# Handing parts of the norms between ScalarE, VectorE, GpSimd and TensorE, and a one-pass second layer norm, in a two-block transformer kernel

## The reference

```python
# block 1, per layer (mod is made from c by ada_w and ada_b)
h = rmsnorm(x, norm_mix_g[l]) * (1.0 + sc1) + sh1
u = h @ w_in[l]
...
x = x + g1 * (mix @ w_out[l])
h = rmsnorm(x, norm_ffn_g[l]) * (1.0 + sc2) + sh2
f = (jax.nn.silu(h @ ffn_w1[l]) * (h @ ffn_w3[l])) @ ffn_w2[l]
x = x + g2 * f
...
# after block 1
x = rmsnorm(x, final_g)
# block 2, per layer
h = x @ w_in[i]
...
x = layer_norm(ALPHA * x + mix, ln1_g[i], ln1_b[i])
gate, up = jnp.split(x @ w_ffn_in[i], 2, axis=-1)
ffn = (jax.nn.silu(gate) * up) @ w_ffn_out[i]
ple = (p[i] @ w_ple[i]) * jax.nn.sigmoid(x @ w_ple_gate[i])
x = layer_norm(ALPHA * x + ffn + ple, ln2_g[i], ln2_b[i])
```

## Time and profile before

| | us |
|---|---|
| time of the kernel before, median of 3 runs | 2750.97 (2750.26 to 2753.71) |
| the profiled execution, its own time | 2746.25 |
| span of that execution in the profile | 2744.5 |
| PE busy (share of the span) | 2579.8 (94%) |
| POOL busy | 1126.8 (41%) |
| DVE busy | 1019.1 (37%) |
| ACT busy | 893.6 (33%) |

### The profile page before, as it was taken

The page is one execution under the profiler, slowest core; times in us unless marked ns, Lnnn a source line. Parts: engine busy times, 40 slices in busy tenths (PEclk is TensorE's granted clock), DMA queues, the critical chain, the costliest instruction groups (busy, mean ns, idle before and its releaser), DMA issues.

```text
span 2744.5 us, 30543 instructions
## 1 busy us (share of the span) xinstructions
PE 2579.8 (94%) x11680; PEld 2029.1 (74%) x11680; DVE 1019.1 (37%) x1750; ACT 893.6 (33%) x1177; POOL 1126.8 (41%) x388
## 2 busy tenths in 40 slices
PE   6897799999999779999989989999989998999998
PEld 4673688878776468887878668887868776888785
DVE  5683710039675560000059543000026846100002
ACT  4224332222423342222243553232124364222212
POOL 1332345544333225554425335555342633455441
PEclk8998899999999889999999999999999999999998
DMA  7511423257420333222322112322341211322231
GB/s 262 184 48 46 160 78 100 92 151 224 135 90 31 107 108 107 92 87 85 101 82 79 53 62 93 106 93 77 95 116 48 84 45 64 101 97 92 83 94 53
DMA packets 309325, 267.76 MB, mean 98 GB/s; under 512 B 20104, under 2 KB 298360, under 8 KB 308984
## 3 DMA queue, kind: packets, MB, share of 16 engines
q1 hardware_dynamic: 309240, 266.63, 30.9%
HBM read 264.51 MB, written 2.10 MB: 97 GB/s over the span
## 4 chain that ended last, share of the span: by engine, by line
PE 85%; DVE 5%; ACT 3%; issue 3%; POOL 2%; DMA 1%; SPq 1%; DVEq 0%; ACTq 0%; POOLq 0%
PE bank L2106 25%; PE bank L2108 25%; PE bank L2107 25%; POOL w_lo L1301 1%; PE bank L2200 1%; PE bank L2440 1%; PE bank L2350 1%; PE bank L2319 1%; PE bank L2506 1%; DMA z_a<-in_ada_w 1%; ACT w_hi L808 1%; DMA raw<-in_ffn_w 1%; PE bank L2539 1%; PE bank L2366 1%; DVE b_acc L1525 0%
## 5 line engine op out<-in xcount | busy, mean ns | idle before, releaser
L1301 POOL TENSOR_TENSOR w_lo<-raw,w_hi 128x2048 fp32r<-128x2048 f32 (+1 forms) x216 | 915.4, 4238 | 1188.6 <-ACT w_hi L808 1162.2
L2106 PE MATMUL bank<-h_hi,w_lo 128*128 128x512 f32 (+1 forms) x2192 | 871.2, 397 | 58.6 <-DVE h_lo L1590 25.1
L2107 PE MATMUL bank<-h_lo,w_hi 128*128 128x512 f32 (+1 forms) x2192 | 862.0, 393 | 0.0
L2108 PE MATMUL bank<-h_hi,w_hi 128*128 128x512 f32 (+1 forms) x2192 | 861.7, 393 | 0.0
L2106 PEld LDWEIGHTS bank<-h_hi,w_lo 128*128 128x128 f32 (+1 forms) x2192 | 416.4, 190 | 163.3 <-issue 55.0
L808 ACT ACTIVATE w_hi<-raw 128x2048 fp32r<-128x2048 f32 (+1 forms) x216 | 378.1, 1750 | 478.0 <-PE bank L2108 449.6
L2108 PEld LDWEIGHTS bank<-h_hi,w_hi 128*128 128x128 f32 (+1 forms) x2192 | 415.9, 190 | 89.7 <-issue 0.4
L2107 PEld LDWEIGHTS bank<-h_lo,w_hi 128*128 128x128 f32 (+1 forms) x2192 | 417.2, 190 | 87.1 <-issue 1.1
L1630 DVE TENSOR_TENSOR f_full<-f_act,bank 128x512 f32<-128x512 f32 x88 | 60.5, 688 | 883.8 <-PE bank L2108 883.8
L2106 PE MATMUL bank<-f_hi,w_lo 128*128 128x512 f32 x704 | 280.7, 399 | 13.3 <-POOL f_lo L1313 13.3
L2108 PE MATMUL bank<-f_hi,w_hi 128*128 128x512 f32 x704 | 280.8, 399 | 0.0
(11 more groups left out here) (305 smaller groups left out, 2455.4 us busy)
## 6 DMA issues: line engine op xcount, KB each, us to landing
raw<-in_ffn_w SPq DMA_DIRECT2D x44, 1024.0 KB
raw<-in_w_ffn_in SPq DMA_DIRECT2D x44, 1024.0 KB
raw<-in_w_in SPq DMA_DIRECT2D x34, 1024.0 KB
raw<-in_ffn_w SPq DMA_DIRECT2D x32, 704.0 KB
raw<-in_w_ffn_out SPq DMA_DIRECT2D x32, 704.0 KB
b_raw<-in_ada_w SPq DMA_DIRECT2D x16, 1024.0 KB, 5.1
a_raw<-in_ada_w SPq DMA_DIRECT2D x32, 512.0 KB, 4.7
z_a<-in_ada_w SPq DMA_DIRECT2D x4, 2048.0 KB, 13.3
```

The costliest lines, as they stand in the source:

```text
L1301: pool.tensor_tensor(b.w_lo[p][:, 0:n], b.raw[p][:, 0:n], b.w_hi[p][:, 0:n].bitcast(F32), ALU.subtract)\
L2106: pe.matmul(out, wlo, xhi, start=start, stop=False)
L2107: pe.matmul(out, whi, xlo, start=False, stop=False)
L2108: return pe.matmul(out, whi, xhi, start=False, stop=stop)
```

## The change

What follows names parts by letters.

(a) The counting semaphore of the low halves is now one for each slot, so that two engines can make them. At five norms, the `w_lo` of the unit p = 1 of the pair that follows is made by DVE (`dve_split`) and no longer by POOL: at the mid norm of each layer of block 1, at the end of each of its layers (where the next layer or block 2 begins), and at the end of layer 0 of block 2. POOL keeps p = 0.

(b) In the RMS norms DVE squares the last tile (`dve_square`) and ACT only tiles 0 to 6, so ACT's split of the unit p = 1 no longer stands behind a square.

(c) DVE no longer adds the last square; TensorE adds it by a second product with ones that accumulates in the same bank (`pe_rms`).

(d) The full value of tile 0 is made by DVE (`dve_full`, in layer norms `dve_normed`) and no longer by ACT.

(e) At the start of layer 1 of block 1, TensorE does the two parameter transposes first, then 4 of the 16 one-column products of part 0, then the two products of the norm, then the other 12 and the 16 of part 1.

(f) In ln1, TensorE adds the last tile into the mean by a second product; DVE adds up only to tile 6.

(g) ln2 is made in one pass (`dve_shift_norm`, `act_shift_norm`, `pe_shift_sums`, `pe_shift_norm`). After tile 3, DVE's sum goes to TensorE, and every tile is shifted by 2/D times that sum, a guess of the mean. The squares of the shifted tiles are made on ACT and summed on DVE while TensorE still multiplies w2. After the last tile, TensorE adds the last tile to the sum and the last square to the sum of squares, and the variance is the mean square less the square of the mean. The tiles are centred after that, each before it is scaled. The eight products over squares of line 2440 are gone for ln2. TensorE's loop over w2 is written out for its last half in block 2 (`down`), with one product with ones inside and two before the last unit.

Waits of a few operations on their own engine are counted on fewer semaphores; the instructions stay the same there.

```diff
-        self.lo = up("lo", 0, 2)
+        self.lo = [up(f"lo{p}", 0, 1) for p in range(2)]
...
         act.activation(b.h_hi[:, k, :], b.sq[:, k, :], ACT.Identity, bias=bias, scale=gain[:, k:k + 1])\
            .then_inc(s.hh.up, 1)
-        act.activation(full[:, k, :], b.sq[:, k, :], ACT.Identity, bias=bias, scale=gain[:, k:k + 1])\
-           .then_inc(s.hf.up, 1)
+        if k:
+            act.activation(full[:, k, :], b.sq[:, k, :], ACT.Identity, bias=bias, scale=gain[:, k:k + 1])\
+               .then_inc(s.hf.up, 1)
...
-        if i == 7:
-            act_next(act, e, after, 0)
-        act_square(act, e, l * 2 + 2, i, w2_square(b, i), lay.bank_out(i % 2, Q_W2 + i // 2))
-        if i == 7:
-            act_next(act, e, after, 1)
+        if i < 7:
+            act_square(act, e, l * 2 + 2, i, w2_square(b, i), lay.bank_out(i % 2, Q_W2 + i // 2))
+        else:
+            for p in range(2):
+                act_next(act, e, after, p)
...
+def act_shift_norm(act, e, l, low):
+
+    s, b, bank = e.s, e.b, e.bank
+    act.wait_ge(*s.n2_mean(l, 2))
+    act.activation(b.f_full[:, 1, :], bank[6][:, :], ACT.Square, scale=1.0 / D).then_inc(s.n2_r.up, 1)
+    act.wait_ge(*s.n2_var(l, 1))
+    act.activation(b.r[:, :], b.f_full[:, 1, :], ACT.Ln, bias=b.eps[:, 1:2]).then_inc(s.n2_r.up, 1)
+    act.wait_ge(*s.n2_r(l, 2))
+    act.activation(b.r[:, :], b.r[:, :], ACT.Exp, scale=-0.5).then_inc(s.n2_r.up, 1)
+    act_normed(act, e, l * 2 + 1, 16, low)
...
+def dve_square(dve, e, k, out, ready):
+
+    dve.wait_ge(*ready)
+    dve.tensor_tensor(out, e.b.x[:, k, :], e.b.x[:, k, :], ALU.mult).then_inc(e.s.ssq.up, 1)
+
+
+def dve_split(dve, e, u):
 
     s, b = e.s, e.b
-    dve.wait_ge(*s.r(c, 1))
+    dve.wait_ge(*s.hi_in(u, 1))
+    dve.tensor_tensor(b.w_lo[1][:, :], b.raw[1][:, :], b.w_hi[1][:, :].bitcast(F32), ALU.subtract)\
+       .then_inc(s.lo[1].up, 1)
+
+
+def dve_full(dve, e, c, gain, shift, full):
+
+    s, b = e.s, e.b
+    dve.wait_ge(*s.xr(c, KD if c == 0 else 1))
+    if shift is None:
+        op = dve.tensor_scalar(full[:, 0, :], b.sq[:, 0, :], gain[:, 0:1], None, ALU.mult)
+    else:
+        op = dve.tensor_scalar(full[:, 0, :], b.sq[:, 0, :], gain[:, 0:1], shift[:, 0:1], ALU.mult, ALU.add)
+    op.then_inc(s.xr.up, 1)
...
+def dve_shift_norm(dve, e, lay, l, low):
+
+    s, b, bank = e.s, e.b, e.bank
+    turn = 2 * DEPTH + 1 + l
+
+    def take(k):
+        dve.wait_ge(*s.tile(lay.pair(20 + k), 1, 1))
+        if k >= 5:
+            dve.wait_ge(*s.n2_d(l, k + 1))
+        dve.tensor_tensor(b.x[:, k, :], bank[k % 2][:, :], b.x[:, k, :], ALU.add).then_inc(s.bank[k % 2].up, 1)
+
+    def add_up(k, first, n):
+
+        if k == first:
+            dve.tensor_tensor(b.r[:, :], b.x[:, 0, :], b.x[:, 1, :], ALU.add).then_inc(s.n2_sum.up, 1)
+        else:
+            dve.wait_ge(*s.n2_sum(l, n))
+            dve.tensor_tensor(b.r[:, :], b.r[:, :], b.x[:, k, :], ALU.add).then_inc(s.n2_sum.up, 1)
+
+    def shift(k):
+        if k < 5:
+            dve.wait_ge(*lay.bank_out(k % 2, Q2_W2 + k // 2))
+        dve.scalar_tensor_tensor(b.x[:, k, :], bank[6][:, :], -2.0 / D, b.x[:, k, :], ALU.mult, ALU.add)\
+           .then_inc(s.n2_d.up, 1)
+
+    def centre(k):
+        dve.scalar_tensor_tensor(b.x[:, k, :], bank[6][:, :], -1.0 / D, b.x[:, k, :], ALU.mult, ALU.add)\
+           .then_inc(s.n2_c.up, 1)
+
+    def squares(k):
+        dve_rms_sum(dve, e, turn, k, b.f_full[:, 0, :], w2_square(b, k))
+
+    for k in range(5):
+        take(k)
+        if 1 <= k < 4:
+            dve.wait_ge(*lay.bank_out(k % 2, Q2_W2 + k // 2))
+            add_up(k, 1, k - 1)
+    dve.wait_ge(*s.n2_mean(l, 1))
+    for k in range(KD):
+        shift(k)
+    for k in range(1, 5):
+        dve.wait_ge(*s.n2_d(l, k + 1))
+        squares(k)
+        add_up(k, 1, k + 2)
+    for k in range(5, KD - 1):
+        take(k)
+        dve.wait_ge(*lay.bank_out(k % 2, Q2_W2 + k // 2))
+        add_up(k, 1, k + 2)
+        squares(k)
+    take(KD - 1)
+    dve_square(dve, e, KD - 1, w2_square(b, KD - 1), lay.bank_out(1, Q2_W2 + 3))
+    if low:
+        dve_split(dve, e, Layer(s, 2, l + 1).pair(0))
+    dve.wait_ge(*s.n2_r(l, 1))
+    dve.wait_ge(*s.rms(turn, 1))
+    dve.scalar_tensor_tensor(b.f_full[:, 1, :], bank[7][:, :], 1.0 / D, b.f_full[:, 1, :], ALU.mult, ALU.subtract)\
+       .then_inc(s.n2_var.up, 1)
+    for k in range(2):
+        centre(k)
+    dve.wait_ge(*s.n2_r(l, 3))
+    for k in range(KD):
+        dve.wait_ge(*s.n2_c(l, k + 1))
+        dve_scaled(dve, e, k)
+        if k == 0:
+            dve_normed(dve, e, l * 2 + 1, 16)
+        if k + 2 < KD:
+            centre(k + 2)
+        if low and k > 1:
+            dve_normed_low(dve, e, l * 2 + 1, k - 2)
+    if low:
+        dve_normed_low(dve, e, l * 2 + 1, KD - 2)
+        dve_normed_low(dve, e, l * 2 + 1, KD - 1)
...
-def pe_rms(pe, e, c, total):
+def pe_rms(pe, e, c, total, last):
     s, b = e.s, e.b
+    pe.wait_ge(*s.ssq(c, 7 if c == 0 else 6))
+    pe.matmul(e.bank[7][:, :], b.ones[:, :], total, start=True, stop=False)
     pe.wait_ge(*s.ssq(c, 7))
-    pe.matmul(e.bank[7][:, :], b.ones[:, :], total, start=True, stop=True).then_inc(s.rms.up, 1)
+    pe.matmul(e.bank[7][:, :], b.ones[:, :], last, start=False, stop=True).then_inc(s.rms.up, 1)
...
+    with pe.Fori(0, 4 if lay.blk == 1 else 2) as i:
         for m in range(2):
-            for p in range(2):
-                u = lay.pair(i * 2 + (j0 // 2 + 11 + m))
-                pe.wait_ge(*s.lo_in(u, p))
-                if p == 0:
-                    pe.wait_ge(*lay.bank_free(m, i + q))
-                for k in range(11):
-                    op = three(pe, bank[m][:, :], w11(b.w_hi[p])[:, k, :], w11(b.w_lo[p])[:, k, :],
-                               b.f_hi[:, 11 * p + k, :], b.f_lo[:, 11 * p + k, :], p == 0 and k == 0,
-                               p == 1 and k == 10)
-                op.then_inc(s.half.up, 2)
+            down(i, m)
+    if lay.blk == 2:
+        down(2, 0)
+        pe.wait_ge(*s.n2_sum(lay.l, 3))
+        pe.matmul(bank[6][:, :], b.ones[:, :], b.r[:, :], start=True, stop=True).then_inc(s.n2_mean.up, 1)
+        down(2, 1)
+        down(3, 0)
+        down(3, 1, lambda: pe_shift_sums(pe, e, lay.l))
...
-        add_partitions(0)
         parameters()
-        pe_rms(pe, e, c, b.f_full[:, 0, :])
+        add_partitions(0, 0, 4)
+        pe_rms(pe, e, c, b.f_full[:, 0, :], w2_square(b, KD - 1))
+        add_partitions(0, 4, 16)
         pe.wait_ge(*s.mod(l, 1))
-        add_partitions(1)
+        add_partitions(1, 0, 16)
...
-    pe.wait_ge(*s.lsum(c, 7))
-    pe.matmul(bank[6][:, :], b.ones[:, :], b.r[:, :], start=True, stop=True).then_inc(s.lmean.up, 1)
+    pe.wait_ge(*s.lsum(l, 6))
+    pe.matmul(bank[6][:, :], b.ones[:, :], b.r[:, :], start=True, stop=False)
+    pe.wait_ge(*s.res(l, KD))
+    pe.matmul(bank[6][:, :], b.ones[:, :], b.x[:, KD - 1, :], start=False, stop=True).then_inc(s.lmean.up, 1)
...
+def pe_shift_sums(pe, e, l):
+    s, b, bank = e.s, e.b, e.bank
+    pe.wait_ge(*s.n2_sum(l, 9))
+    pe.matmul(bank[6][:, :], b.ones[:, :], b.r[:, :], start=True, stop=False)
+    pe.wait_ge(*s.ssq(2 * DEPTH + 1 + l, 6))
+    pe.matmul(bank[7][:, :], b.ones[:, :], b.f_full[:, 0, :], start=True, stop=False)
+
+
+def pe_shift_norm(pe, e, lay, l):
+    s, b, bank = e.s, e.b, e.bank
+    pe.wait_ge(*lay.bank_out(1, Q2_W2 + 3))
+    pe.matmul(bank[6][:, :], b.ones[:, :], b.x[:, KD - 1, :], start=False, stop=True).then_inc(s.n2_mean.up, 1)
+    pe.wait_ge(*s.ssq(2 * DEPTH + 1 + l, 7))
+    pe.matmul(bank[7][:, :], b.ones[:, :], w2_square(b, KD - 1), start=False, stop=True).then_inc(s.rms.up, 1)
```

256 lines of the change are left out of this document (151 added, 105 removed).

## The result

The first comparison, four runs of each kernel, gave 2723.68 us (2719.23 to 2727.11) for the changed kernel and 2750.61 (2748.77 to 2753.71) for the kernel before, 26.9 us less; the ratio is 0.990, with an interval from 0.9883 to 0.9917. I had forecast 2738.5, with a range from 2732 to 2746. The profiled executions differ less: a span of 2725.3 against 2744.5, 19.2 us.

A forecast was written before the change was run, and what follows sets the result against it. TensorE, busy 94% of the span, was taken as the bound, so only what ends its idle time counts. Terms 0.7 + 2.1 + 2.9 + 3.2 - 3.1 + 1.3 + 1.1 + 4.3 = 12.5 gave median 2738.5, range 2732 to 2746.

The forecast's parts named there:

- first norm of all: First norm of the kernel: DVE makes tile 0's full value beside its high half, so the low half follows at once; +0.7.
- mid norm, layer 0: Block 1: the first root ends at 338.4 against 340.5 with the low-half split on DVE; 2.1 us gained.
- start of layer 1: Block 1: 24 one-column rows now follow the norm's products, taking 4.1 us, so the first product comes later; 3.1 us lost.
- mid norm, layer 1: Block 1: root at 999.8 against 1002.7, no longer held by GpSimd's split; 2.9 us gained.
- between the blocks: Norm between blocks 1 and 2: ACT's split starts earlier, TensorE starts at 1383.7 and not 1386.88; 3.2 us gained.
- ln2, layer 0: Block 2: eight products with ones and eight centrings leave the path, but DVE's queue before the low half grows; +1.1.
- ln2, layer 1, and output: End of block 2: the eight products, 9.97 us at half clock, go; ACT's last tile ends at 2731.0 against 2735.34; +4.3.
- The first rival: Start of layer 1, block 1, loses nothing: +1.2 or near 0 in place of -3.1, 2734 to 2735.5; chance 0.16.
- The 0.8 that I took off at ln2: Block 2, layer 0: TensorE idles 8.7 us and not 4.6, so a longer half-clock stretch was charged 0.8 us.
- The clock rival: At eight TensorE restarts half clock lasts 3.5 us longer, 1.75 lost each, 14 in all: 2752, no change; chance 0.10.
- I carry the gain over to the median unchanged: Gain of 12.5, reckoned on one execution of 2746.25, was taken off the runs' median of 2750.97, giving 2738.5.
- the slower rival: Block 2's w2 loop starves: DVE held, ACT's splits late, TensorE waits, 18 us in each layer: 2756, slower; chance 0.04.

The follow-up runs named there:

- The second profile of the kernel before: Kernel before, unedited, timed against itself: 2745.27, ratio to itself 0.9997; this profile has a span of 2743.0 and 197.4 us at half clock.
- the 67 later ones: Single executions of the kernel before, unedited, in all comparisons after the first: 2731 to 2754, median 2744.6.
- fillers: Products that nothing reads, added in TensorE's waits: to the kernel before 2737.99; to the changed kernel 2726.51 with 8 and 14, 2719.39 with 5, 5, 5, 9, 4.

## Why the prediction was wrong

The second profile of the kernel before and the first of the changed one have nearly the same half-clock stretches until the first mid norm and start the same products within 0.02 us of each other from 60 us on until there, so their difference by place is the fairest test of the terms. They differ by 17.7 us in span.

| place | forecast | measured |
|---|---|---|
| first norm of all | +0.7 | 0.0 |
| mid norm, layer 0 | +2.1 | +2.7 |
| start of layer 1 | -3.1 | +0.2 |
| mid norm, layer 1 | +2.9 | +3.3 |
| between the blocks | +3.2 | +3.5 |
| ln1, both layers | +1.3 | +1.6 |
| ln2, layer 0 | +1.1 | +2.4 |
| ln2, layer 1, and output | +4.3 | +4.0 |
| sum | 12.5 | 17.7 |

**The direction and the mechanisms at the norms were right.** The split's price (2.28), the held sum, the roots at 0.69 and the longer way to the low half in ln2 are all in the rows. The experiments that undo (a) and (b) cost by medians what the steps say (10.3 and 4.7), though by place (a) costs more and (b) is spread otherwise. At the mid norm of layer 0 the first product itself comes 2.1 earlier, the forecast to the tenth; the other 0.5 comes in the ten us behind it, from fewer products at half clock.

**"Start of layer 1, -3.1" was mis-sized, by 3.3 us.** The sum assumed that the 24 rows behind the norm run partly at half clock (4.1 us) and that the wait for `a_acc` grows by 0.5. The rows took 2.73, and in the kernel before the rows of part 0 can fall to half clock themselves (4.68 for 32, where I had 3.63). The place also has back 0.5 us of clock behind the first product. The way from the FFN's last product to the first one of layer 1 grows by 0.4 to 1.9 us, by which execution of before is taken. The first rival, that this place loses nothing, is what the fair pair shows, but not for its reason: the 32 rows of part 1 still take 6.35.

**The clock was left out of the sum, except for 0.8 taken off.** I had costed only what an idle TensorE loses. The changed kernel idles less at the mid norms and between the blocks and then spends less time at half clock, 25 us on average. In the fair pair, the stretches at half clock at both mid norms, at the start of layer 1 and between the blocks are shorter by 6.8 us each. By place only a little of that is time won: 0.5 to 0.6 us behind the first product at each of these four places, 2.2 in all, and the three norms among them stood at nothing. The 9 to 10 us that the line through the executions gives is not shown to be the clock's share. The 0.8 that I took off at ln2 did not come. The clock rival had the right place and the wrong sign.

**"I carry the gain over to the median unchanged" failed in its base.** The median of three runs, 2750.97, was itself 6.4 above the median of the 67 later ones. My 12.5 under 2744.6 would have been 2732.1; the changed kernel's own median over 16 runs is 2726.8. So of the 14.8 us between 2738.5 and 2723.68, 6.4 were the base, 5.3 the terms (three fifths of these the start of layer 1), and 3.1 the difference of the first four runs of the changed kernel from all sixteen. This account takes the first comparison for a chance one of the same kind as the later ones. Within it the kernel before stood at 2750.61, where I had put it, and it was the gain, 26.9 for 12.5, that was off.

**(g) was not under-costed but over-costed.** Undone alone it costs 2.3 by medians and 2.4 by profiles, against the 4.1 that my terms leave for it. Three products in the w2 loop take 2.6, as forecast (2.7). The 9.97 us that the sum gave to the eight products of the last ln2, which the earlier trace rows don't show, is this row of the kernel before:

```profile
2717.47 9.97 PE L2440 MATMUL bank<-m_sq,ones 128*128 128x512 f32 x16 [1.45 <-ACT m_sq L1076]
```

**Open.** Why the scores of either layer run at half clock in some executions and not in others is not settled, nor how much of the 26.9 us of the first comparison was chance, nor why fillers bring the kernel before only 2.6 by medians. Parts (c), (d) and (f) were never undone alone, so their share is argued from the rows. A hold of VectorE in block 2's w2 loop, the slower rival, does not show: TensorE's waits for `w_lo` are 6.7 us in 7 before and after.

## What to carry to other kernels

When an engine's wait ends on a chain of small operations, write out every operation of the chain in the order of each engine, and look for one with two SBUF inputs beside a GpSimd operation: here it lasted to the end of GpSimd's operation wherever in the chain it stood, and moving it only moved the hold. Before a forecast of half a percent, look at how far single executions lie apart, on more than one chip, and at whether they line up with the granted clock; three runs and one profile could not carry it here. A line through executions says what goes together and not what a change will bring; for that, compare two profiles by place. And where TensorE has to wait some microseconds, count the clock behind the wait, or fill the wait with products that nobody reads, measured so that they end before it does.

## What the hardware showed that I had not expected

Executions of one kernel, over the chips used, spread over 23 us (2731 to 2754), nearly in a straight line with the time at half clock, 0.39 us for each us. A product of 512 float32 columns by a matrix of ones takes 0.88 us of TensorE at full clock when several follow each other (16 rows in 7.03). And in the changed kernel the clock fell to half (at 718.0) while TensorE was in the one-column products at the start of layer 1: 0.114 us a row before it (24 in 2.73) and 0.198 (32 in 6.35) over the group in which it fell, with only 0.27 of waiting between.
